# Gate and up products of the FFN by one level of Strassen's seven-product scheme, in a float32 decoder layer on one NeuronCore

## The chip, the cores and the metric

The kernel runs on one NeuronCore of a Trainium2 chip. The metric is the device time of one execution in microseconds; the number given for a kernel is the median of its runs. The engines of the core are TensorE (PE in the profile), VectorE (DVE), ScalarE (ACT), GpSimd (POOL) and SyncE (SP), which issues most of the DMAs. Each runs its own program, and they wait for each other by semaphores. Times of the profile are counted from the start of its span.

## The reference, cut to what matters

One layer of a decoder with 512 prompt tokens and 8 sample tokens, D_MODEL = 2048 and D_FF = 5632:

```python
def layer_out(h, o_sb, o_cm, p, g_out_sb, g_out_cm, w_out, g_ffn, w_gate, w_up, w_down,
              g_ple, w_ple_gate, w_ple_proj):
    ...
    h = h + o @ w_out
    f = rmsnorm(h, g_ffn)
    h = h + (jax.nn.silu(f @ w_gate) * (f @ w_up)) @ w_down
    h = h + jax.nn.sigmoid(rmsnorm(h, g_ple) @ w_ple_gate) * (p @ w_ple_proj)
    return h
```

Ahead of it stand an input projection, a stick-breaking attention group (with 8 x 1024 cached positions) and a gating group, called the mixer here. The change leaves their work as it is. `p` has 256 features.

## The kernel before

**Layout.** All activations lie feature-major: `h`, `x_hi` and `x_lo` are 128 x 16 x 520, that is KT = 16 k-tiles of 128 features by TOK = 520 tokens, which are taken as two halves of HALF = 260. A float32 product is made of three float32r products, `w_hi`·`x_hi`, `w_hi`·`x_lo` and `w_lo`·`x_hi`; the high part is a copy on ScalarE rounded to float32r, the low part a subtraction on VectorE.

**Weights** come in units of 16 blocks of 128 x 128 (1 MB). SP loads them into `w_raw` (two slots), ScalarE makes `w_hi` by halves (`split_w`, `high_w`, L611), VectorE `w_lo` (`low_w`, L868). A unit is 16 blocks x 3 terms x 2 token halves = 96 matmuls of 260 columns (L1214) on TensorE (`unit`), which go into `out_ps`, two tiles in turn (`tile_ps`), each of two PSUM banks, one for each token half. A tile is taken off before the tile after the next starts (`out_read`).

**Order of the program.** Units 0 to 55 are the mixer and the output projection, whose results VectorE adds to `h` (L985). TensorE then sums the squares of `h` over the features by four matmuls with `ones` (`sum_features`, L1253) from `h_sum`, which POOL has added up (L591); this gives `h_r`, the reciprocal root. The FFN has 11 chunks of four 128-feature tiles: per chunk 8 units gate and up, 4 units down (16 output tiles of 4 blocks, 24 matmuls each). The chunks are shifted: the gate and up units of a chunk stand ahead of the down units of the chunk before. The first chunk's gate and up and the last chunk's down are written out, the ten between are a hardware loop of 5 iterations of 24 units on each engine (`Fori`).

**Gate and up** use `h`·gain as operand; VectorE multiplies the finished tile by `h_r` (`take_loop`, L1131) into `y_gate` and `y_up`, ScalarE makes silu, VectorE the product and `act_lo` (`gate_up`). **Down:** VectorE adds each tile to `h` in SBUF (`down_tile`, L1156). **After the FFN** two units multiply `p` (proj, 16 tiles of two blocks), which VectorE copies to SBUF. Then 16 units form the PLE gate, each taken by VectorE (L892), put through the sigmoid, multiplied by proj (L1202), added to `h` (L1203) and stored (`y_t`, L478). While the last down tiles come, VectorE makes the operand of the gate from them (`low_x`), so that between two tiles it has one addition and at times a `low_w` and a `low_x`.

## Time and profile before

| | us |
|---|---|
| median of 3 runs | 2661.23 |
| lowest and highest run | 2659.47, 2663.26 |
| profiled execution, its own time | 2663.89 |
| span of the profiled execution | 2662.3 |
| mean granted clock of TensorE, share of full speed | 0.994 |

The profile is of one execution: a page with the busy time of each engine and its costliest groups, the chain of work that ended last followed back from the end, every instruction with its start and length, and the idle time ahead of it with the instruction that ended it (`<-`). 2663.89 less 2662.3 leaves 1.6 us outside the span. The granted clock is that of TensorE alone; 0.50 is 1.2 GHz and 1.00 is 2.4 GHz.

### The profile page before, as it was taken

Reading aid. Unit: us, or ns where it says so; the run is one execution under the profiler, and the core shown is the slowest. Engines: PE = TensorE matmul, PEld = TensorE weight load, DVE = VectorE, ACT = ScalarE, POOL = GpSimd, SP = SyncE. Lnnn points to the kernel's source line nnn. Section 1 sums busy time; section 2 is a strip of 40 time slices with the busy share of each in tenths; the row PEclk is TensorE's granted clock in tenths of the full one; section 3 lists DMA queues with packets and bytes.
Section 4 is the critical chain, followed back from the end, with each engine's and each line's share of the span. In section 5 each row is a group of like instructions: output and inputs, shape, how many; then the busy total and the mean of one; then the engine's idle time right before and its main releaser. Section 6 shows DMA issues by size and latency. Waiting matters only on the chain.

```text
span 2662.3 us, 49219 instructions
## 1 busy us (share of the span) xinstructions
PE 2623.2 (99%) x21484; PEld 2600.7 (98%) x21484; DVE 1218.7 (46%) x1400; ACT 781.3 (29%) x912; POOL 158.2 (6%) x170
## 2 busy tenths in 40 slices
PE   7999999999999999999999999999999999999999
PEld 6998999999999999999999999999999999999999
DVE  6368776554456533333333333334343424346443
ACT  5544434444523322222122212121212121224221
POOL 4001111110111200000000000000000000003000
PEclk9998999999999999999999999999999999999999
DMA  4255565554332222222222222222222222222223
GB/s 177 95 190 190 215 237 207 175 186 160 108 128 100 84 96 95 85 91 96 96 82 93 96 80 96 96 96 81 95 96 92 93 86 96 94 83 94 96 86 106
DMA packets 57389, 309.18 MB, mean 116 GB/s; under 512 B 7770, under 2 KB 7770, under 8 KB 30178
## 3 DMA queue, kind: packets, MB, share of 16 engines
q1 hardware_dynamic: 47826, 272.50, 29.0%
q0 software_dynamic: 9216, 33.56, 3.6%
q8 instruction: 177, 2.90, 0.4%
q14 instruction: 26, 0.21, 0.0%
q10 hardware_dynamic: 144, 0.01, 0.0%
HBM read 297.46 MB, written 8.59 MB: 115 GB/s over the span
## 4 chain that ended last, share of the span: by engine, by line
PE 95%; DVE 3%; DMA 1%; ACT 1%; issue 1%; SPq 0%; DVEq 0%; ACTq 0%
PE out_ps L1214 87%; PE out_ps L1336 4%; PE pair_ps L1253 1%; DVE w_lo L868 1%; DVE k_ring L899 0%; PE tok_ps L1321 0%; DVE dot_s L900 0%; DMA q_rows<-q_rows_dram 0%; DMA h<-x_t 0%; ACT x_hi L622 0%; PE pair_ps L1284 0%; PE pair_ps L1303 0%; PE tok_ps L1317 0%; PE pair_ps L1290 0%; PE pair_ps L1299 0%
## 5 line engine op out<-in xcount | busy, mean ns | idle before, releaser
L1214 PE MATMUL out_ps<-x_hi,w_hi 128*128 128x260 f32 x5184 | 1066.9, 287 | 25.8 <-DVE w_lo L868 10.0
L1214 PE MATMUL out_ps<-x_hi,w_lo 128*128 128x260 f32 x5184 | 1048.6, 284 | 0.0
L1214 PE MATMUL out_ps<-x_lo,w_hi 128*128 128x260 f32 x5184 | 1046.8, 284 | 0.0
L1214 PEld LDWEIGHTS out_ps<-x_hi,w_hi 128*128 128x128 f32 x5184 | 805.8, 190 | 31.8 <-DVE w_lo L868 8.9
L1214 PEld LDWEIGHTS out_ps<-x_hi,w_lo 128*128 128x128 f32 x5184 | 803.6, 189 | 0.0
L1214 PEld LDWEIGHTS out_ps<-x_lo,w_hi 128*128 128x128 f32 x5184 | 801.4, 189 | 0.0
L611 ACT ACTIVATE w_hi<-w_raw 128x1024 fp32r<-128x1024 f32 x412 | 411.7, 1047 | 590.2 <-PE out_ps L1214 590.2
L868 DVE TENSOR_TENSOR w_lo<-w_raw,w_hi 128x1024 fp32r<-128x1024 f32 x410 | 501.4, 1255 | 125.1 <-ACT w_hi L611 123.7
L1214 PE MATMUL out_ps<-act_hi,w_lo 128*128 128x260 f32 x1408 | 283.9, 283 | 0.0
L1214 PE MATMUL out_ps<-act_lo,w_hi 128*128 128x260 f32 x1408 | 283.3, 283 | 0.0
L1214 PE MATMUL out_ps<-act_hi,w_hi 128*128 128x260 f32 x1408 | 283.2, 282 | 0.0
L1156 DVE TENSOR_TENSOR h<-h,out_ps 128x520 f32<-128x520 f32 x176 | 122.3, 695 | 228.2 <-PE out_ps L1214 228.1
L1214 PEld LDWEIGHTS out_ps<-act_hi,w_lo 128*128 128x128 f32 x1408 | 217.1, 188 | 0.0
L1214 PEld LDWEIGHTS out_ps<-act_hi,w_hi 128*128 128x128 f32 x1408 | 217.1, 188 | 0.0
L1214 PEld LDWEIGHTS out_ps<-act_lo,w_hi 128*128 128x128 f32 x1408 | 216.6, 188 | 0.0
L1131 DVE TENSOR_TENSOR y_up<-out_ps,h_r 128x520 f32<-128x520 f32 x44 | 30.8, 700 | 295.6 <-PE out_ps L1214 295.6
L1131 DVE TENSOR_TENSOR y_gate<-out_ps,h_r 128x520 f32<-128x520 f32 x44 | 30.8, 700 | 285.0 <-PE out_ps L1214 285.0
L818 ACT ACTIVATE act_hi<-y_up 128x520 fp32r<-128x520 f32 x44 | 28.1, 639 | 428.2 <-DVE y_up L1148 428.2
L815 ACT ACTIVATE y_gate<-y_gate 128x520 f32<-128x520 f32 x44 | 28.1, 640 | 381.5 <-DVE y_gate L1131 381.5
L593 POOL COPY h_sum<-h_sq 128x520 f32<-128x520 f32 x2 | 1.8, 902 | 1543.8 <-ACT h_sq L691 1543.8
L1336 PEld LDWEIGHTS out_ps<-a_s,v_ring 128*128 128x128 f32 x688 | 82.1, 195 | 0.0
L1336 PE MATMUL out_ps<-a_s,v_ring 128*128 128x1 f32 x688 | 80.7, 247 | 0.0
(175 smaller groups left out, 1366.0 us busy)
## 6 DMA issues: line engine op xcount, KB each, us to landing
w_raw<-w_units SPq DMA_DIRECT2D x205, 1024.0 KB, 4.8
k_ring<-cache_k SPq DMA_DIRECT2D x50, 512.0 KB, 5.2
v_ring<-cache_v POOLq DMA_DIRECT2D x43, 512.0 KB, 4.5
acc<-cache_v POOLq DMA_DIRECT2D x21, 512.0 KB, 4.8
k_third<-cache_k SPq DMA_DIRECT2D x14, 512.0 KB, 4.5
h<-x_t SPq DMA_DIRECT2D x4, 1040.0 KB, 9.5
y_t<-h SPq DMA_DIRECT2D x16, 260.0 KB, 6.5
q_rows<-q_rows_dram SPq DMA_DIRECT2D x8, 512.0 KB, 5.4
```

Of the source, the lines that this page charges most:

```text
L593: ins = pool.tensor_copy(h_sum[:, :], h_sq[:, 0, :])
L611: act.activation(w_hi[:, u % 2, cols], w_raw[:, u % 2, cols], ACT.Copy).then_inc(hi_done, 1)
L815: act.activation(y_gate[:, :], y_gate[:, :], ACT.Silu).then_inc(silu_done, 1)
L818: act.activation(act_hi[:, par, g, :], y_up[:, :], ACT.Copy).then_inc(act_hi_done, 1)
L868: dve.tensor_tensor(w_lo[:, u % 2, cols], w_raw[:, u % 2, cols], w_hi[:, u % 2, cols], ALU.subtract).then_inc(lo_done, 1)
L1131: dve.tensor_tensor(halves(dst), tile_ps(t), halves(h_r[:, :]), ALU.mult).then_inc(out_read, 1)
L1156: dve.tensor_tensor(halves(h[:, m, :]), halves(h[:, m, :]), tile_ps(t), ALU.add)\
L1214: mm = pe.matmul(out_ps[:, 2 * (t % 2) + a, 0:HALF], w[:, u % 2, cols], x[:, a * HALF:(a + 1) * HALF], start=first and n == 0, stop=last a ...
L1253: mm = pe.matmul(pair_ps[:, a, 0:HALF], ones[:, :], x[:, a * HALF:(a + 1) * HALF], start=True, stop=True)
L1336: mm = pe.matmul(o_s_ps(u)[:, hd:hd + 1], v_slot(j)[:, hd * P:(hd + 1) * P], a_s[:, b % 3, at:at + 1], start=False, stop=j == pages[-1], s ...
```

## The change

**Products.** Two output tiles (2 x 128 features) of gate or up, the two halves of K (8 k-tiles each) and the two token halves form a 2 x 2 by 2 x 2 block product. It is made with seven block products in place of eight (Winograd's form). One block product is 8 k-tiles x 3 terms = 24 matmuls of 260 columns; a pair of tiles takes 168 matmuls where it took 192, and there are 44 pairs (22 gate, 22 up). `product` issues one, `pair_of_tiles` on each engine one pair. Their results go into six single PSUM banks (`gate_acc`, `up_acc`), all matmuls of a product into one bank.

**Operands.** The seven token operands (`ops` 0 to 6, high and low parts of 128 x 8 x 260) stay in SBUF through the FFN. They are built once, from `f` = `h`·gain (ScalarE), multiplied by `h_r` (`scale_op`), combined (`combine_op`), rounded (`high_op`) and subtracted (`low_op`). The weight operands are made anew for each pair: VectorE adds four half units (`add_weights`) and makes seven low parts, ScalarE seven high parts, four copies of a partial result (`copy_part`) and VectorE three additions (`join`). Weights now go by half units ("jobs", four half slots of `w_hi` and `w_lo`); a third raw slot, `w_extra`, is added. The second load of a pair waits for the sums of the pair before, since sums are made in place.

**Residual.** `h` gives its place in SBUF to operands. SP stores it tile by tile to `h_dram` during the last 8 units of the output projection and after them. Each down tile of the first ten chunks is copied by ScalarE into one of four `staging` buffers and added to `h_dram` by a DMA that POOL issues with `accum_op=ALU.add` (160 of 128 x 520 float32, 260 KB). Ahead of the last down, `h` comes back in four loads of 1040 KB, and VectorE adds the last chunk's tiles to it in SBUF.

**Projection** of `p`: its 16 tiles (192 matmuls) move ahead of the FFN; ScalarE copies each to one of two `staging` buffers, POOL stores it to `proj_dram`, and it is loaded back in two halves for the PLE gate.

**Also:** `h_r` comes from Ln and Exp instead of Sqrt and a reciprocal, and ScalarE's table sets are loaded ahead in more places and 28 times instead of 89. The loop has one chunk an iteration: ten iterations on TensorE instead of five.

The diff, cut:

```diff
+            for k in range(KT - 2, KT):
+                keep_h(k)
+            def after_low(job, it=0):
+                sp.wait_ge(lo_done, it * CHUNK_JOBS + (JOB0 + job + 1 - POOL_LO))
+            def after_sums(pair, it=0):
+                sp.wait_ge(w_summed, it * 16 + 4 * (pair + 1))
...
+            sp.wait_ge(ended, LAST_DOWN.end - 2)
+            for i in range(STAGES):
+                sp.wait_ge(h_added[i], 64 * (FFN_CHUNKS - 1))
+            for i in range(4):
+                tiles = slice(4 * i, 4 * i + 4)
+                sp.dma_start(h[:, tiles, :], h_dram[:, tiles, :]).then_inc(h_back[i], 16)
...
+            for n in range(KT):
+                pool.wait_ge(proj_taken, n + 1)
+                pool.dma_start(proj_dram[:, n, :], staging[:, n % 2, :]).then_inc(proj_out[n % 2], 16)
+            for c in range(FFN_CHUNKS - 1):
+                for m in range(KT):
+                    pool.wait_ge(staged, c * KT + m + 1)
+                    pool.dma_start(h_dram[:, m, :], staging[:, m % STAGES, :], accum_op=ALU.add)\
+                        .then_inc(h_added[m % STAGES], 16)
...
+            def take_proj(n):
+                act.wait_ge(ended, n + 1)
+                if n >= 2:
+                    act.wait_ge(proj_out[n % 2], 16 * (n // 2))
+                act.activation(halves(staging[:, n % 2, :]), tile_ps(n), ACT.Copy).then_inc(proj_taken, 1)
...
+            def down_tiles(item, after, it):
+                for j in range(2 * FFN_GROUP):
+                    for t in range(2 * j, 2 * j + 2):
+                        after_end(item.end + t + 1, it)
+                        if t >= STAGES:
+                            act.wait_ge(h_added[t % STAGES], it * 64 + 16 * (t // STAGES))
+                        act.activation(halves(staging[:, t % STAGES, :]), tile_ps(t), ACT.Copy).then_inc(staged, 1)
+                    if j < 4:
+                        high_of(item, j + 4, it)
+                    else:
+                        high_of(after, j - 4, it)
...
+            high_of(first, 1)
+            for g in range(2):
+                high_op(2, g, quad(0, 0, g), 8)
+                take_proj(8 + g)
+            take_proj(10)
+            take_proj(11)
+            high_of(first, 2)
+            for i in range(STAGES):
+                act.wait_ge(h_kept[i], 64)
+            for g in range(2):
+                high_op(3, g, quad(1, 0, g), 12)
+                take_proj(12 + g)
...
+            for j in range(2 * FFN_GROUP):
+                after_end(LAST_DOWN.end + 2 * j + 2)
+                if j < 4:
+                    high_of(LAST_DOWN, j + 4)
+                else:
+                    high_gate(j - 4)
+                for k in range(2 * j, 2 * j + 2):
+                    act.wait_ge(taken, k + 1)
+                    split(x_hi[:, k, :], h[:, k, :], gain_ple[:, k:k + 1])
                     if k >= 2:
-                        split(x_hi[:, k, :], h[:, k, :], gain_ple[:, k:k + 1])
-                    square_residual(KT, k)
-            split_w(U_PROJ + 1)
...
+                    if stage:
+                        low_raw(item.job + stage - 1, item.load + (stage - 1) // 2, (stage - 1) % 2, it)
+                elif stage == 0:
+                    dve.wait_ge(*landed(item.load + 1, it))
+                    after_low(item.job - 2, it)
+                    add_weights(w_sum[:, :], half_of(item.load + 1, 0), half_of(item.load + 1, 1))
+                elif stage == 1:
+                    low_raw(item.job, item.load, 0, it)
+                elif stage == 2:
+                    low(item.job + 1, w_sum[:, :], it)
+                    dve.wait_ge(w_summed, it * 16 + (4 * item.pair + 1))
+                    add_weights(half_of(item.load + 1, 0), half_of(item.load, 0), half_of(item.load + 1, 0))
+                    after_low(item.job + 1, it)
+                    add_weights(w_sum[:, :], w_sum[:, :], half_of(item.load, 0))
+                elif stage == 3:
+                    low(item.job + 2, w_sum[:, :], it)
...
-            def down_tile(t, m, it=0):
-                dve.wait_ge(out_done, it * (2 * CHUNK_TILES) + (t + 1))
-                dve.wait_ge(out_read, it * (2 * CHUNK_TILES) + t)
-                dve.tensor_tensor(halves(h[:, m, :]), halves(h[:, m, :]), tile_ps(t), ALU.add)\
-                    .then_inc(out_read, 1)
...
+                dve.wait_ge(ended, it * CHUNK_ENDS + (item.end + 4))
+                dve.wait_ge(copied, it * 16 + (4 * item.pair + 1))
+                join(part[:, 0, :], part[:, 0, :], y_acc)
+                prepare(after, 1, it)
+                dve.wait_ge(copied, it * 16 + (4 * item.pair + 4))
+                join(part[:, 2, :], part[:, 2, :], part[:, 3, :])
+                prepare(after, 2, it)
...
+            def scale_op(half_k, half_t, g):
+                x = quad(half_k, half_t, g)
+                r = h_r[:, half_t * HALF:(half_t + 1) * HALF].unsqueeze(1).to_broadcast([P, 4, HALF])
+                dve.tensor_tensor(x, x, r, ALU.mult).then_inc(op_built, 1)
...
+            first = FIRST[0]
+            prepare(first, 0)
+            dve.wait_ge(root_done, 4)
+            dve.wait_ge(f_done, KT)
+            for g in range(2):
+                scale_op(0, 0, g)
...
+            for j in range(2 * FFN_GROUP):
+                if j < 4:
+                    low_raw(LAST_DOWN.job + j + 4, LAST_DOWN.load + (j + 4) // 2, j % 2)
+                else:
+                    low_gate(j - 4)
+                for k in range(2 * j, 2 * j + 2):
+                    if k % 4 == 0:
+                        dve.wait_ge(h_back[k // 4], 16)
+                    dve.wait_ge(ended, LAST_DOWN.end + k + 1)
+                    dve.tensor_tensor(halves(h[:, k, :]), halves(h[:, k, :]), tile_ps(k), ALU.add).then_inc(taken, 1)
+                    if k:
+                        low_x(k - 1, h[:, k - 1, :], gain_ple[:, k - 1:k])
...
+            def product(job, op, acc, fresh, it=0):
+                after_low(job, it)
+                hi, lo = ops[op]
+                for g in range(GROUPS):
+                    if job < FIRST[1].job and g % 4 == 0:
+                        pe.wait_ge(op_lo_done, 2 * op + g // 4 + 1)
+                    cols = slice(g * P, (g + 1) * P)
+                    w_h, w_l = half_slot(w_hi, job)[:, cols], half_slot(w_lo, job)[:, cols]
+                    for n, (w, x) in enumerate(((w_h, hi), (w_h, lo), (w_l, hi))):
+                        mm = pe.matmul(acc, w, x[:, g, :], start=fresh and g == 0 and n == 0,
+                                       stop=g == GROUPS - 1 and n == 2, skip_group_check=True)
+                mm.then_inc(ended, 1)
...
+                    pe.wait_ge(up_read if up else gate_read, it * 2 + turn_of)
+                    pe.wait_ge(joined, it * 12 + 3 * (item.pair - 1))
+                product(item.job, 0, x_acc, True, it)
+                product(item.job + 1, 1, z_acc, True, it)
+                pe.wait_ge(copied, it * 16 + (4 * item.pair + 1))
+                product(item.job + 2, 2, x_acc, False, it)
+                product(item.job + 3, 3, y_acc, True, it)
+                pe.wait_ge(copied, it * 16 + (4 * item.pair + 3))
+                product(item.job + 4, 4, x_acc, False, it)
+                product(item.job + 5, 5, z_acc, False, it)
+                pe.wait_ge(copied, it * 16 + (4 * item.pair + 4))
+                product(item.job + 6, 6, x_acc, False, it)
...
+            pe.wait_ge(p_lo_done, 2)
+            for n in range(KT):
+                job = n // 4
+                if n % 4 == 0:
+                    after_low(job)
+                if n < 2:
+                    pe.wait_ge(out_read, T_FFN - 1 + n)
+                else:
+                    pe.wait_ge(proj_taken, n - 1)
+                for k in range(2):
+                    plain_block(job, n % 4 * 2 + k, tile_ps(n), p_hi[:, k, :], p_lo[:, k, :], k == 0, k == 1)
+                if n == 2:
                     sum_features(h_sum, h_sum_done, KT, (root_done, 4)).then_inc(x_sum_ready, 1)
...
-            with pe.Fori(0, (FFN_CHUNKS - 1) // 2) as it:
-                for half in range(2):
-                    u0 = U_LOOP + half * CHUNK_UNITS
-                    for x in range(2 * FFN_GROUP):
-                        unit(u0 + x, 1, ffn_operand, it=it)
-                    pe.wait_ge(act_lo_done, it * (2 * FFN_GROUP) + FFN_GROUP * (1 + half))
...
+            with pe.Fori(0, FFN_CHUNKS - 1) as it:
+                g0, down, u0, g1, u1 = LOOP
+                pair_of_tiles(g0, gate_acc, it)
+                pe.wait_ge(act_lo_done, it * 2 + 2)
+                pe.wait_ge(joined, it * 12 + 3 * (g0.pair))
+                down_tiles(down, lambda t: pe.wait_ge(staged, it * KT + (t - 1)) if t >= 2 else None, it)
+                pe.wait_ge(staged, it * KT + KT)
+                pair_of_tiles(u0, up_acc, it)
+                pair_of_tiles(g1, gate_acc, it)
+                pair_of_tiles(u1, up_acc, it)
+            pe.wait_ge(act_lo_done, 2 * FFN_CHUNKS)
+            pe.wait_ge(joined, 3 * 4 * FFN_CHUNKS)
```

VectorE's order where the FFN begins; `w_lo`, `op_lo` and `f` are the low parts of weights and operands and the residual times gain. Before:

```order
L985 TENSOR_TENSOR h<-h,sq 128x520 [waits out_read]
L877 SCALAR_TENSOR_TENSOR x_lo<-h,gain_ffn,x_hi 128x520 [waits x_hi_done,h_final]
L877 SCALAR_TENSOR_TENSOR x_lo<-h,gain_ffn,x_hi 128x520 [waits x_hi_done] x7
L868 TENSOR_TENSOR w_lo<-w_raw,w_hi 128x1024 [waits hi_done] x2
L882 RECIPROCAL h_r<-h_r 128x520 [waits root_done]
L1131 TENSOR_TENSOR y_gate<-out_ps,h_r 128x520 [waits out_done,r_done]
L868 TENSOR_TENSOR w_lo<-w_raw,w_hi 128x1024 [waits hi_done] x2
```

After the change:

```order
L1351 TENSOR_TENSOR h<-h,sq 128x520 [waits out_read]
L1234 TENSOR_TENSOR w_lo<-w_raw,w_hi 128x1024 [waits hi_done,h_final]
L1234 TENSOR_TENSOR w_lo<-w_raw,w_hi 128x1024 [waits hi_done]
L1512 TENSOR_TENSOR w_sum<-w_raw 128x1024 [waits lo_done,w_in0]
L1591 TENSOR_TENSOR f<-f,h_r 128x4x260 [waits f_done,root_done]
L1591 TENSOR_TENSOR f<-f,h_r 128x4x260 x3
L1499 TENSOR_TENSOR w_lo<-w_extra,w_hi 128x1024 [waits hi_done]
L1603 TENSOR_TENSOR op_lo<-f,op_hi 128x1040 [waits op_hi_done] x2
L1596 SCALAR_TENSOR_TENSOR f<-f 128x4x260 [waits op_built] x2
L1591 TENSOR_TENSOR f<-f,h_r 128x4x260 x2
L1603 TENSOR_TENSOR op_lo<-f,op_hi 128x1040 [waits op_hi_done] x2
L1499 TENSOR_TENSOR w_lo<-w_sum,w_hi 128x1024 [waits hi_done]
```

Between the last addition to `h` and the steady work stood eight `x_lo`, a unit's two low parts and the reciprocal; now the same place holds the building of the seven operands (instructions on `f` and `op_lo`) with the weight work of the first pair between them.

VectorE in the last down phase, from its first `w_lo`. Before:

```order
L868 TENSOR_TENSOR w_lo<-w_raw,w_hi 128x1024 [waits hi_done]
L1156 TENSOR_TENSOR h<-h,out_ps 128x520 [waits out_read,out_done]
L868 TENSOR_TENSOR w_lo<-w_raw,w_hi 128x1024 [waits hi_done]
L1156 TENSOR_TENSOR h<-h,out_ps 128x520 [waits out_read,out_done] x3
L877 SCALAR_TENSOR_TENSOR x_lo<-h,gain_ple,x_hi 128x520 [waits x_hi_done]
L868 TENSOR_TENSOR w_lo<-w_raw,w_hi 128x1024 [waits hi_done]
L1156 TENSOR_TENSOR h<-h,out_ps 128x520 [waits out_read,out_done]
L877 SCALAR_TENSOR_TENSOR x_lo<-h,gain_ple,x_hi 128x520 [waits x_hi_done]
```

After the change:

```order
L1499 TENSOR_TENSOR w_lo<-w_raw,w_hi 128x1024 [waits hi_done]
L1676 TENSOR_TENSOR h<-h,out_ps 128x520 [waits ended,h_back0]
L1676 TENSOR_TENSOR h<-h,out_ps 128x520 [waits ended]
L1243 SCALAR_TENSOR_TENSOR x_lo<-h,gain_ple,x_hi 128x520 [waits x_hi_done]
L1499 TENSOR_TENSOR w_lo<-w_raw,w_hi 128x1024 [waits hi_done]
L1676 TENSOR_TENSOR h<-h,out_ps 128x520 [waits ended]
L1243 SCALAR_TENSOR_TENSOR x_lo<-h,gain_ple,x_hi 128x520 [waits x_hi_done]
L1676 TENSOR_TENSOR h<-h,out_ps 128x520 [waits ended]
L1243 SCALAR_TENSOR_TENSOR x_lo<-h,gain_ple,x_hi 128x520 [waits x_hi_done]
```

A `w_lo` now stands ahead of every two additions to `h` to the end of the phase, each made when ScalarE has the high part (`hi_done`).

TensorE at the end of a down phase in the loop, its last block and the next gate or up product. Before:

```order
L1214 MATMUL out_ps<-act_lo,w_hi 128x260 x2
L1214 MATMUL out_ps<-act_hi,w_lo 128x260 x2
L1226 REGISTER_ALU
L1233 REGISTER_ALU [waits lo_done]
L1214 MATMUL out_ps<-x_hi,w_hi 128x260 [waits out_read]
```

After the change:

```order
L1919 MATMUL out_ps<-act_lo,w_hi 128x260 x2
L1919 MATMUL out_ps<-act_hi,w_lo 128x260 x2
L1995 REGISTER_ALU
L1911 REGISTER_ALU [waits joined,up_read,staged]
L1934 MATMUL mix_ps<-op_hi,w_hi 128x260 [waits lo_done]
```

The first matmul of the next product waited for the tile before the last one to be taken (`out_read`, a count); now a register instruction ahead of it waits for all sixteen staging copies (`staged`).

## Rows read from the trace of the kernel before

**Rows 1.** The page: busy time of each engine (part 1).
```profile
PE 2623.2 (99%) x21484; PEld 2600.7 (98%) x21484; DVE 1218.7 (46%) x1400; ACT 781.3 (29%) x912; POOL 158.2 (6%) x170
```

**Rows 2.** The chain that ended last, from 915 us: start, length, what.
```profile
914.99 12.12 PE out_ps L1214 x101
927.11 0.88 PE pair_ps L1253 x4
...
2472.31 184.53 PE out_ps L1214 x1536
```

**Rows 3.** VectorE in order of time as the FFN begins (start, duration).
```profile
916.42 0.70 DVE L985 TENSOR_TENSOR h<-h,sq 128x520 f32<-128x520 f32 x1
...
951.16 0.70 DVE L1131 TENSOR_TENSOR y_gate<-out_ps,h_r 128x520 f32<-128x520 f32 x1 [6.15 <-PE out_ps L1214]
953.52 2.36 DVE L868 TENSOR_TENSOR w_lo<-w_raw,w_hi 128x1024 fp32r<-128x1024 f32 x2 [1.66 <-ACT w_hi L611]
...
974.23 0.70 DVE L1131 TENSOR_TENSOR y_gate<-out_ps,h_r 128x520 f32<-128x520 f32 x1 [6.15 <-PE out_ps L1214]
```

**Rows 4.** Busy time in stretches (columns in its first line): loop turns, after two waits.
```profile
core 0: us, PE busy (x) PEld busy (x) DVE busy (x) ACT busy (x) POOL busy (x), PEclk, DMA share, GB/s
1275.00:1295.00 20.00, 18.44 (x154) 18.24 (x154) 7.51 (x8) 3.08 (x4) 0.00 (x0) 1.00 0.31 107
1555.00:1575.00 20.00, 18.21 (x140) 18.01 (x139) 6.29 (x8) 2.00 (x2) 0.00 (x0) 0.91 0.31 107
...
52.00:53.00 1.00, 1.00 (x6) 1.00 (x6) 0.00 (x0) 0.24 (x1) 0.00 (x0) 0.50 0.00 0
...
55.00:56.00 1.00, 1.00 (x10) 1.00 (x10) 0.00 (x0) 0.00 (x0) 0.00 (x0) 1.00 0.00 0
...
253.00:254.00 1.00, 1.00 (x5) 1.00 (x6) 0.93 (x3) 0.00 (x0) 0.00 (x0) 0.50 0.07 16
262.00:263.00 1.00, 1.00 (x7) 1.00 (x6) 0.50 (x1) 0.00 (x0) 0.00 (x0) 0.50 0.98 295
```

**Rows 5.** TensorE in order of time: matmuls that followed a wait (last bracket).
```profile
50.42 0.48 PE L1214 MATMUL out_ps<-x_hi,w_hi 128*128 128x260 f32 x2 [2.33 <-DVE y L892]
...
252.92 1.10 PE L1265 MATMUL tok_ps<-ident,vg 128*128 128x128 f32 x4 [2.99 <-DVE vg L1064]
...
1287.08 0.50 PE L1214 MATMUL out_ps<-x_hi,w_hi 128*128 128x260 f32 x2 [1.56 <-DVE h L1156]
```

**Rows 6.** VectorE, groups of instructions by line and shape: busy us, mean ns.
```profile
L868 DVE TENSOR_TENSOR w_lo<-w_raw,w_hi 128x1024 fp32r<-128x1024 f32 x410 | 501.4, 1255 | 125.1 <-ACT w_hi L611 123.7
...
L886 DVE SCALAR_TENSOR_TENSOR q<-y,gain_q,sq 128x520 f32<-128x520 f32 x8 | 6.1, 760 | 38.8 <-ACT sq L636 38.8
...
L999 DVE TENSOR_TENSOR x_sq<-x_sq 128x1040 f32<-128x1040 f32 x4 | 5.0, 1239 | 0.1
...
L972 DVE TENSOR_TENSOR z<-z,mix_ps 128x256 f32<-128x256 f32 x8 | 3.4, 420 | 0.3
```

**Rows 7.** VectorE late in the last down phase (in order of time).
```profile
2415.95 1.56 DVE L868 TENSOR_TENSOR w_lo<-w_raw,w_hi 128x1024 fp32r<-128x1024 f32 x1 [1.60 <-ACT w_hi L611]
2417.43 0.68 DVE L1156 TENSOR_TENSOR h<-h,out_ps 128x520 f32<-128x520 f32 x1
```

**Rows 8.** ScalarE, groups by line, 850 to 1010 us.
```profile
L611 ACT ACTIVATE w_hi<-w_raw 128x1024 fp32r<-128x1024 f32 x26 | 26.0, 1048 | 38.6 <-PE out_ps L1214 38.6
...
L815 ACT ACTIVATE y_gate<-y_gate 128x520 f32<-128x520 f32 x4 | 2.6, 638 | 27.9 <-DVE y_gate L1131 27.9
...
L627 ACT ACTIVATE h_r<-pair_ps,eps 128x520 f32<-128x520 f32 x1 | 0.7, 697 | 4.4 <-PE pair_ps L1253 4.4
```

**Rows 9.** The page: DMA issues, median us to landing (part 6).
```profile
w_raw<-w_units SPq DMA_DIRECT2D x205, 1024.0 KB, 4.8
```

**Rows 10.** Landing times of the 16 y_t stores and of the 8 k_t stores.
```profile
DMA to landing us min/median/max: 2.0/6.5/7.1
...
DMA to landing us min/median/max: 6.2/6.7/8.1
```

More of the change, by code:

```diff
@@ L57 @@
 U_GATE = U_PROJ + 2
-UNITS = U_GATE + KT
 T_OUT = U_OUT
@@ new lines, in _ @@
+            for i in range(2):
+                sp.wait_ge(proj_out[i], 16 * HEADS)
+            sp.wait_ge(ended, LAST_DOWN.end)
+            sp.dma_start(proj[:, 0:HEADS, :], proj_dram[:, 0:HEADS, :]).then_inc(proj_in_done[0], 16)
+            for i in range(LAST_DOWN.load + 3, GATE_LOAD + KT):
+                after_low(LAST_DOWN.job + 2 * (i - RAW_SLOTS - LAST_DOWN.load) + 1)
+                load(i, U_LAST_DOWN + 3 if i < GATE_LOAD else U_GATE + i - GATE_LOAD)
+                if i == GATE_LOAD + 2:
+                    sp.wait_ge(ended, GATE_END)
+                    sp.dma_start(proj[:, HEADS:KT, :], proj_dram[:, HEADS:KT, :]).then_inc(proj_in_done[1], 16)
@@ new lines, in high_op, with after_end, high, high_raw @@
+            def high_op(i, g, src, built_at):
+                act.wait_ge(op_built, built_at + g + 1)
+                act.activation(ops[i][0][:, 4 * g:4 * g + 4, :], src, ACT.Copy).then_inc(op_hi_done, 1)
+            def after_end(end, it=0):
+                act.wait_ge(ended, it * CHUNK_ENDS + end)
+            def high(job, src):
+                act.activation(half_slot(w_hi, job), src, ACT.Copy).then_inc(hi_done, 1)
+            def high_raw(job, i, half, it=0):
+                act.wait_ge(*landed(i, it))
+                high(job, raw(i)[:, half * GROUPS * P:(half + 1) * GROUPS * P])
@@ new lines, in half_of, with add_weights, prepare @@
+            def half_of(i, half):
+                return raw(i)[:, half * GROUPS * P:(half + 1) * GROUPS * P]
+            def add_weights(dst, x, w):
+                dve.tensor_tensor(dst, x, w, ALU.add).then_inc(w_summed, 1)
+            def prepare(item, stage, it=0):
+                if isinstance(item, Down):
+                    if stage:
[14 more added lines that the diff above has]
+                    low(item.job + 2, w_sum[:, :], it)
+                else:
+                    low_raw(item.job + 3, item.load, 1, it)
+                    after_low(item.job + 2, it)
+                    add_weights(w_sum[:, :], w_sum[:, :], half_of(item.load, 1))
@@ L1218, in block_products, with unit @@
                     mm.then_inc(out_done, 1)
-            def unit(u, tiles, operand, each=None, it=0, between={}):
+            def unit(u, tiles, operand, each=None, between={}):
                 per = SLOTS // tiles
@@ new lines, in plain_block @@
+            def plain_block(job, b, tile, hi, lo, first, last):
+                cols = slice(b * P, (b + 1) * P)
+                w_h, w_l = half_slot(w_hi, job)[:, cols], half_slot(w_lo, job)[:, cols]
+                for n, (w, x) in enumerate(((w_h, hi), (w_h, lo), (w_l, hi))):
+                    for a in range(2):
+                        mm = pe.matmul(tile[:, a, :], w, x[:, a * HALF:(a + 1) * HALF],
+                                       start=first and n == 0, stop=last and n == 2)
+                if last:
+                    mm.then_inc(ended, 1)
```

707 lines of the change are left out of this document (503 added, 204 removed).

## Prediction

> **What bounds the kernel now.** I read the page's busy times first: TensorE is busy 2623.2 of 2662.3 us, VectorE 46% and ScalarE 29% [rows 1]. The chain that ended last then names matmuls nearly throughout, one stretch without a break being 1536 matmuls in 184.53 us, 120.1 ns each [rows 2]. So what leaves TensorE's program leaves the time, and what makes TensorE wait is added. Last come the stretches around its few waits: a turn of the loop costs 1.56 us [rows 5], and after a wait the granted clock can stand at half (1.2 GHz) for a while [rows 4]. The times below are on the profiled execution, 2663.9 us with 1.6 outside the span.
>
> **Removed.** 44 pairs lose 24 matmuls each, 1056 x 120.1 ns = **126.9 us**. Down, gate and the 192 matmuls of proj stay as many. That a matmul costs the same when all of a product go into one bank is not shown before, where two banks alternate; the nearest row, four alternating matmuls in 0.88 us, tells little [rows 2], so I take 120.1 for both. A bound: 5 ns either way on the 7392 matmuls of the products would be 37 us. I see no reason for either sign.
>
> The Trainium skill (TensorE: Matmul & The Clock Gate, Back-to-back issue gap) gives N/2.4 + 2.5 ns for an isolated matmul of N columns, 110.8 ns for 260. The trace has 120.1, so the row decides; by the page the saving would be 117.0.
>
> **Steady work, hidden.** A product is 24 x 0.1201 = 2.88 us, a pair 20.18. VectorE does 11 instructions of 1024 elements per pair; two back to back take 2.36 us [rows 3], 1.18 each, and 1.255 as the group's mean [rows 6]. With three joins near the 256-column row's 0.42 this is 14.2 us for a gate pair. For an up pair come a 520-column product (0.70), two of 260 columns from PSUM (near 0.42) and a 1040-column subtraction (1.24), 17.1 in all [rows 3, 6]. ScalarE has seven highs at 1.05 and four copies, about 10 [rows 8]. Both fit in 20.18, and following the waits product by product I find each low part ready over 4 us early. The third raw slot lets the second load of a pair go at about 4.8 us into the pair before; it lands 4.8 later [rows 9], at 9.6, and is first read at 11.3. Down tiles take 2.88 each; ScalarE needs 2 x 0.65 + 1.05 = 2.35 of 5.77 per two tiles [rows 8]. What this cover lacks: VectorE has only 3 us to spare in an up pair.
>
> **Building the operands: +23.1.** Let 0 be the end of the output projection, 915.6 us in the trace: two units of gate and up lie between the two takes at 951.16 and 974.23, so a unit is 11.53 [rows 3]. TensorE alone would do proj (23.07), the sums (0.88 [rows 2]) and pair 0 (20.18) by 44.1. But VectorE has 38 large instructions (scales, combinations and low parts of 1040 elements, weight sums and low parts of 1024) before product 4 may start. They are near 1.24 and 1.18 each [rows 3, 6], 1.18 taken: 44.8. They begin when the last addition is done (1.5: it starts at 916.42 and takes 0.70 [rows 3]), the root is there (sums at 7.9, Ln and Exp 0.70 and 0.64 like the 520-column rows [rows 8], so 9.3), and the load issued after the last store of h has landed (about 10, two loads of 4.8 in a row [rows 9]); I take 11.1. So low part 4 is ready at 56, products 4 to 6 end at 64.7, and the excess is 20.6. In it TensorE waits twice, near 5 and 7 us, for proj tiles whose copies stand behind ScalarE's `high_op`; after waits of 2.33 and 2.99 us the clock stood at half [rows 4, 5]. I put 2.5 on it. Bounds: at 1.24 each the chain is 2.3 longer, and eight of its instructions do two operations, which at 520 columns take 0.76 [rows 6], twice that 1.52: 2.7 more. If a proj store lands as late as a y_t store in a row of them (7.1 us, 2.0 when alone [rows 10]), two takes cycle in 7.9 and it is +18 more; downwards the two clock losses and a load that lands at 8 allow -4.5.
>
> **Loop turns: +10.** Nine turns instead of four, 1.56 us each [rows 5], and one of the four seen stood at a granted clock of 0.91 over 20 us, the others near 1.00 [rows 4], 1.8 us lost in one of four. So 2.0 each, and five more are 10; 0 to 3 each is the range.
>
> **End of each down phase: +8.** TensorE waits there for the sixteenth staging copy: the copy of 520 columns, 0.64 [rows 8], and the two handovers, 0.8. Ten times. Before, it went on with another tile pair.
>
> **Before the last down: +3.5.** The last up pair's products end, then two short multiplications, a low part ahead of them, ScalarE's high and VectorE's low of the activations (1.24 [rows 6]) must pass before the first down block; part of it overlaps. From 2 to 5.
>
> **The last down: +24.** Before, VectorE's `w_lo` of 1.56 us waited 1.60 for ScalarE's high part and the addition of 0.68 came after it [rows 7]; the slot of that unit was free a unit early. Now ScalarE may write the high part of job j+4 only when tile 2j+1 ends, VectorE's low of it stands ahead of the additions of tiles 2j and 2j+1, and tile 2j+2 waits for the first of these. TensorE's gap is high 1.05 [rows 8], low 1.18 [rows 3], addition 0.70 [rows 3] less overlap, with handovers 3.0. Eight times. Bounds 2.0 and 3.9 each, so 16 and 31.
>
> **The clock after these nine gaps: +14.4.** The nearest rows: after the wait of 2.33 us that ended at 50.42 the clock is 0.50 at 52 to 53 and 1.00 at 55; I read 3.2 us at half, 1.6 lost. After one of 2.99 that ended at 252.92 it is still 0.50 at 262 to 263, some 10 us, 5.1 lost [rows 4, 5]. The gaps here are 3.0 but the work between them, 5.8 us, is dense; and a turn of 1.56 cost nothing three times in four. I take 1.6 each; 0 and 5.1 each are the bounds, 0 and 46.
>
> **Sum:** 23.1 + 10 + 8 + 3.5 + 24 + 14.4 = 83.0 against 126.9, net -43.9: 2663.9 - 43.9 = 2620.0. The profiled run is 2.7 above the median, so **2617** for the median.
>
> **Rivals.**
>
> *The accumulating DMA paces the down phases, slower than before.* Tile t is copied only when the DMA of tile t-4 has landed. With copy and handover 0.7 and landing time L, four slots hold if (0.7 + L)/4 is at most 2.88 us, L at most 10.8 us. ScalarE, waiting for it, also holds back `high_of` queued behind it, and POOL's queue holds only these. The trace has no accumulating DMA. Plain transfers of the same 260 KB landed in 2.0 to 7.1 and the k_t stores in 6.2 to 8.1 [rows 10], which is for the cover. An addition in DRAM reads the old value beside the new one, so as the far end I take twice the row's 7.1, 14.2: a tile then takes 3.73 instead of 2.88: 160 x 0.85 = 136, so 2617 + 136 = **2753**. It turns the result over from L = 11.9, where 160 x 0.27 = 44. Against it: the DMA engines are little used in the FFN, and one DMA at a time was the fast case.
>
> The Trainium skill (Collectives: The Full Stack, The bandwidth ceiling) says that a transfer with an add needs two source reads and runs at half the rate. No row of the kernel before shows whether that holds here.
>
> *The clock stays low, or proj's stores hold the prologue.* Nine gaps at 5.1 instead of 1.6 give +31.5: **2648**. The stores at 7.1 give +18: 2635; both 2667.
>
> *The gaps are smaller.* No clock lost at the nine (-14.4), the last down's gap at 2.0 (-8) and turns of 1.56 as before (-4): **2591**.
>
> *The change doesn't do what it says*, TensorE's count of matmuls not falling by 1056: excluded by the instruction order but for the price of each; 5 ns more on each product matmul gives 2654.
>
> **How the numbers follow.** Main case 0.52, 2595 to 2645. Clock or stores 0.14, 2645 to 2667. Smaller gaps 0.17, 2575 to 2600. Slow accumulating DMA 0.14, 2656 to 2753. The rest 0.03. The range takes in all but the low tail of the third (0.05) and most of the fourth (0.12): 2580 to 2680. The measurement of this kernel tells 0.2% (5.3 us) from no change. Below 2655.9 lie the first, the third and nearly all of the second case: 0.82. Within 0.2%: 0.03. Above 2666.6: 0.15.
>
> **What would show it.** TensorE's matmul records: 1056 fewer, at 120 ns in an unbroken stretch of products. Product 4 of the first pair starting near 56 us after the output projection's end, ended by an `op_lo`. In the loop's down phases, the median landing time of the accumulating DMAs under 10.8, and no TensorE wait released by ScalarE's staging copy but at the end of each. In the last down, eight waits of 3 us released by the addition to h, and the granted clock around them. I am wrong if the pairs in the loop take clearly more than 20.2 us, if the down phases take over 46 + 1 us, or if the loads come late for `add_weights`.

## The result and the profile after

| | before | after |
|---|---|---|
| median, us | 2661.61 (4 runs, 2659.47 to 2663.26) | 2616.66 (4 runs, 2613.26 to 2622.05) |
| profiled execution, its time and span | 2663.89, 2662.3 | 2618.02, 2616.1 |
| mean granted clock | 0.994 | 0.984 |

The ratio of the times is 0.9831, with a 95% interval of 0.9818 to 0.9843: 45 us faster. The forecast was 2617. In the profiled executions the stretch from the end of the output projection to the end of the span shrank by 43.9 us (1746.7 to 1702.8), which is the forecast's net to the digit. That is luck in part: below, the matmuls saved 6 us more than forecast, and the waits with the clock cost 7 more.

The page of the changed kernel, busy time by engine (it answers to [rows 1]):

```profile
PE 2520.4 (96%) x20428; PEld 2492.4 (95%) x20428; DVE 1450.2 (55%) x1588; ACT 1015.5 (39%) x1351; POOL 304.2 (12%) x346
```

TensorE's records fell from 21484 to 20428, by 1056. It is no longer busy all the time: 96% instead of 99%. Its waits, summed by the instruction that waited and the one that released it (us, times, longest):

```profile
PE out_ps L1919 <- DVE h L1676: 24.7, 8, 3.1
PE out_ps L1919 <- ACT staging L1020: 13.1, 7, 5.6
PE pair_ps L1934 <- DVE w_lo L1499: 10.4, 6, 1.9
...
PE mix_ps L1934 <- ACT staging L1117: 7.7, 10, 0.8
...
PE pair_ps L1934 <- issue: 4.4, 3, 1.5
PE out_ps L1919 <- DVE act_lo L1574: 3.6, 1, 3.6
```

These lines are the forecast's terms: eight waits for the addition to `h` in the last down phase, seven for the projection's copies, nine at the turns of the loop (six ended by `w_lo`, three by nothing that shows, "issue"), ten for the sixteenth staging copy, one for `act_lo`. In order of time, TensorE after one wait of each kind (idle time in the last bracket):

```profile
1105.51 0.38 PE L1934 MATMUL mix_ps<-op_hi,w_hi 128*128 128x260 f32 x1 [0.77 <-ACT staging L1117]
...
1167.92 0.38 PE L1934 MATMUL pair_ps<-op_hi,w_hi 128*128 128x260 f32 x1 [1.82 <-DVE w_lo L1499]
...
2337.74 0.51 PE L1919 MATMUL out_ps<-act_hi,w_hi 128*128 128x260 f32 x2 [3.56 <-DVE act_lo L1574]
...
2348.40 0.48 PE L1919 MATMUL out_ps<-act_hi,w_hi 128*128 128x260 f32 x2 [3.10 <-DVE h L1676]
...
2423.54 0.51 PE L1919 MATMUL out_ps<-x_hi,w_hi 128*128 128x260 f32 x2 [3.01 <-DVE h L1676]
```

From 2337.74 to 2423.54 are 85.8 us for 384 matmuls that take 45.88 without a wait. The chain that ended last shows both rates (start, length, what): 72 matmuls of products in 8.62 us are 119.7 ns each, 384 of a down phase in 45.88 are 119.5, and the first product after the turn took 4.66 instead of 2.87:

```profile
1058.87 45.88 PE out_ps L1919 x384
...
1131.63 8.62 PE pair_ps L1934 x72
...
1167.92 4.66 PE pair_ps L1934 x24
```

The granted clock (the column after the busy times of PE, PEld, DVE, ACT and POOL, as in [rows 4]) in that first product, and in a block of the last down phase after its wait:

```profile
1169.00:1171.00 2.00, 2.00 (x11) 2.00 (x11) 2.00 (x3) 0.49 (x1) 0.00 (x0) 0.50 0.00 0
...
2369.70:2372.00 2.30, 2.30 (x11) 2.30 (x12) 1.75 (x3) 2.28 (x4) 1.07 (x1) 0.51 0.03 7
```

### The profile page after: what moved, and what is told of

It is laid out like the page before. It is cut to its first block, busy times and chain, and to the rows that moved or that the text cites. A ratio compares the mean times of both kernels' runs of the same rounds, so it can differ in the third digit from the quotient of the medians.

```text
span 2616.1 us, 48548 instructions
## 1 busy us (share of the span) xinstructions
PE 2520.4 (96%) x20428; PEld 2492.4 (95%) x20428; DVE 1450.2 (55%) x1588; ACT 1015.5 (39%) x1351; POOL 304.2 (12%) x346
## 3 DMA queue, kind: packets, MB, share of 16 engines
q0 software_dynamic: 33536, 80.43, 15.2%
## 4 chain that ended last, share of the span: by engine, by line
PE 90%; DVE 5%; ACT 2%; issue 2%; DMA 2%; SPq 0%; DVEq 0%; POOL 0%; ACTq 0%; POOLq 0%
PE out_ps L1919 27%; PE out_ps L1702 22%; PE pair_ps L1934 12%; PE mix_ps L1934 9%; PE out_ps L1934 7%; PE tok_ps L1934 5%; PE out_ps L1824 4%; PE pair_ps L1741 1%; ACT w_hi L1033 1%; DVE x_lo L1243 1%; DVE w_lo L1499 1%; DVE dot_s L1266 1%; DVE w_lo L1234 1%; DVE k_ring L1265 1%; DMA k_ring<-cache_k 0%
## 5 line engine op out<-in xcount | busy, mean ns | idle before, releaser
L1702 PE MATMUL out_ps<-x_hi,w_hi 128*128 128x260 f32 x1792 | 383.5, 296 | 17.8 <-DVE w_lo L1234 9.6
L1499 DVE TENSOR_TENSOR w_lo<-w_raw,w_hi 128x1024 fp32r<-128x1024 f32 x196 | 239.0, 1223 | 276.6 <-ACT w_hi L1033 276.6
L1702 PE MATMUL out_ps<-x_hi,w_lo 128*128 128x260 f32 x1792 | 364.8, 285 | 0.0
L1702 PE MATMUL out_ps<-x_lo,w_hi 128*128 128x260 f32 x1792 | 364.4, 285 | 0.0
L1702 PEld LDWEIGHTS out_ps<-x_hi,w_hi 128*128 128x128 f32 x1792 | 282.5, 192 | 22.4 <-DVE w_lo L1234 9.1
L1702 PEld LDWEIGHTS out_ps<-x_hi,w_lo 128*128 128x128 f32 x1792 | 280.5, 191 | 0.0
L1702 PEld LDWEIGHTS out_ps<-x_lo,w_hi 128*128 128x128 f32 x1792 | 280.0, 191 | 0.0
L1934 PE MATMUL pair_ps<-op_hi,w_hi 128*128 128x260 f32 x880 | 250.5, 285 | 15.7 <-DVE w_lo L1499 10.4
L1934 PE MATMUL pair_ps<-op_hi,w_lo 128*128 128x260 f32 x880 | 250.5, 285 | 0.0
L1934 PE MATMUL pair_ps<-op_lo,w_hi 128*128 128x260 f32 x880 | 250.0, 284 | 0.0
```

The lines of the kernel that those rows point to most:

```text
L1499: dve.tensor_tensor(half_slot(w_lo, job), src, half_slot(w_hi, job), ALU.subtract)\
L1702: mm = pe.matmul(out_ps[:, 2 * (t % 2) + a, 0:HALF], w[:, u % 2, cols], x[:, a * HALF:(a + 1) * HALF], start=first and n == 0, stop=last a ...
L1934: mm = pe.matmul(acc, w, x[:, g, :], start=fresh and g == 0 and n == 0, stop=g == GROUPS - 1 and n == 2, skip_group_check=True)
```

## The experiments

All are edits of the changed kernel and are compared with its 2616. One thing is needed to read the small effects: the output projection, which no edit touches, ended between 909.3 and 918.4 us of the span in the profiled executions, so a whole time says little about 3 us. For such effects I read stretches inside a trace.

**The changed kernel again.**

> The changed kernel once more, as the reference for the small effects of the runs beside it. Every theory: 2616 +- 4 us, TensorE's waits in the last down phase 8 of 3.1 us, at the end of the loop's down phases 10 of 0.77, at the loop turns 9 of 1.5 to 1.9.

2615.88 (2612.89 to 2621.56, 5 runs). The loop's period, from one wait for the sixteenth copy to the next over nine chunks, was 129.4 us, 129.8 in the first trace. The waits at the turns are as long in both; the granted clock fell after three of the nine turns in the first trace and after one of nine in this one, and each such turn made its period 1.4 to 1.9 us longer.

**Last down phase: additions ahead of the low part (adds_first).**

```diff
             for j in range(2 * FFN_GROUP):
-                if j < 4:
-                    low_raw(LAST_DOWN.job + j + 4, LAST_DOWN.load + (j + 4) // 2, j % 2)
-                else:
-                    low_gate(j - 4)
                 for k in range(2 * j, 2 * j + 2):
...
                     dve.tensor_tensor(halves(h[:, k, :]), halves(h[:, k, :]), tile_ps(k), ALU.add).then_inc(taken, 1)
+                    if k % 2:
+                        if j < 4:
+                            low_raw(LAST_DOWN.job + j + 4, LAST_DOWN.load + (j + 4) // 2, j % 2)
+                        else:
+                            low_gate(j - 4)
```

> In the last down phase VectorE adds tiles 2j and 2j+1 to h before it makes the low part of job j+4, instead of after it. Theory (the order of VectorE's queue makes the gaps): the eight waits of 3.1 us go (24.7), and with them the time at half clock after them. From the changed kernel's trace that stretch lasts 85.8 us from the start of its first block to the first gate block, less 46 of work less 24.7 is 15; one share of it, near 2, stays behind the wait for act_lo. So -38 us: 2579. Rival 1 (the low part is as urgent as the addition): TensorE then waits about 1 us eight times for w_lo, the clock still drops: 2600. Rival 2 (the low clock in this stretch has another cause than the waits): only the 24.7 go: 2592.

2577.16 (2574.77 to 2579.84), 38.7 less. The waits for `h` are gone from TensorE's list; what is left after the loop is the one for `act_lo`:

```profile
PE mix_ps L1935 <- ACT staging L1117: 7.7, 10, 0.8
...
PE out_ps L1920 <- DVE act_lo L1574: 3.6, 1, 3.6
```

24.7 of the 38.7 are the waits, 14 the time at the low clock, which went with them: the stretch of 85.8 us now takes 48.4, and the gate after it 1.6 less. Neither rival holds: no `w_lo` took their place, and the low clock left with the waits, but for the 2.5 us that follow the wait for `act_lo`.

**Fifteen staging copies (staged_15).**

```diff
-                pe.wait_ge(staged, it * KT + KT)
+                pe.wait_ge(staged, it * KT + KT - 1)
```

> TensorE waits at the end of each of the ten down phases for fifteen staging copies instead of sixteen; the banks of tile 14 are those the next product pair uses, tile 15's are not. Theory (the wait is for ScalarE's last copy and nothing else is late there): ten waits of 0.77 go and 0.1 each with them: 2608. Rival (the next product's low part or ScalarE's up_read is as late): under 2 us, 2615.

2605.60 (2601.97 to 2612.75), 10.3 less than the run beside it (2615.88), where the theory had 8 and the rival under 2. The waits for the copies are gone from the list, and the loop's shortest period fell from 129.1 to 128.1 us: 1.0 for each wait of 0.77. The other 0.3 is not the clock, which stood at 1.00 after all ten of these waits; what it is was not tried.

**TensorE's loop written out (no_loop).**

```diff
-            with pe.Fori(0, FFN_CHUNKS - 1) as it:
+            for it in range(FFN_CHUNKS - 1):
```

> TensorE's loop over ten chunks is written out (about 10,000 more matmuls in its program); the other engines keep their loops. Theory (a turn costs TensorE 1.5 to 1.9 us, and some turns a stretch at half clock): the iterations took 129.1 us, five of them 131, so 9 x 1.6 and 5 x 1.9 go, 24: 2593. Rival 1 (the wait at the turn is VectorE's w_lo, which the trace names as releaser in five of nine): the wait stays there, about 1 us five times, 2602. Rival 2 (a long straight program starves TensorE for instructions): 2616 or more.

2597.06 (2594.22 to 2598.59), 18.8 less, 5 short of the theory and as far from the first rival. The trace decides between them: no wait is left at the former turns, and the period is flat.

```profile
1236.28 0.39 PE L1934 MATMUL mix_ps<-op_hi,w_hi 128*128 128x260 f32 x1 [0.69 <-ACT staging L1117]
...
1363.58 0.39 PE L1934 MATMUL mix_ps<-op_hi,w_hi 128*128 128x260 f32 x1 [0.69 <-ACT staging L1117]
```

127.29 us apart, as all nine are. Against the 129.43 of the run beside it that is 2.1 us a turn and 19.3 in all, which is the 18.8 measured; against the 129.79 of the first trace, with two more turns at the low clock, it is 2.5 and 22.5. The theory had taken five long turns of nine; the first trace has three and the run beside it one. So `w_lo`, which the trace named as releaser at most turns, was not what TensorE lacked there, and rival 1 falls. And a straight program of some 10,000 matmuls is fed without a wait.

**The projection ahead of the operands (proj_early).**

```diff
-                pool.dma_start(proj_dram[:, n, :], staging[:, n % 2, :]).then_inc(proj_out[n % 2], 16)
+                pool.dma_start(proj_dram[:, n, :], staging[:, n % 3, :]).then_inc(proj_out[n % 3], 16)
...
+            for n in range(8, 11):
+                take_proj(n)
             high_of(first, 1)
+            for n in range(11, 14):
+                take_proj(n)
             for g in range(2):
                 high_op(2, g, quad(0, 0, g), 8)
-                take_proj(8 + g)
-            take_proj(10)
-            take_proj(11)
+                take_proj(14 + g)
```

> The sixteen tiles of p's projection go through three staging buffers instead of two, and ScalarE copies tiles 8 to 15 ahead of the high parts of operands 2 to 4 instead of between them. From the end of the output projection the first down phase began 145.5 to 146.4 us later in five runs of kernels with the old order. Theory (VectorE's chain of 38 instructions, which ended 55.5 us after that point, ties with TensorE's delayed projection): TensorE's waits of 13 us and most of the time at half clock move to a wait for VectorE's low parts, and the stretch shortens by about 1 us: 144.5, the whole 2615. Rival (the stores and ScalarE's copies alone hold this stretch, as the chain of waits reads): it shortens by the 13 us of waits and some 5 us of clock, 128 us, the whole 2598.

2615.32 (4 runs), and the stretch from the end of the output projection (909.8) to the first down phase (1059.7) took 150.0 us, 4.5 more than before the edit. TensorE's waits for the projection's copies fell from 13.1 to 7.4 us, but now it waited 11.8 at product 2, for ScalarE's copy of an earlier result (`part`). That copy stood in ScalarE's queue behind the last high parts of the operands, which waited 4.49 us for VectorE's `op_lo`. And VectorE's chain was 3.5 us longer, since ScalarE's high part of job 1 stood behind the copies I had moved. First VectorE, then ScalarE and TensorE:

```profile
939.86 1.23 DVE L1499 TENSOR_TENSOR w_lo<-w_sum,w_hi 128x1024 fp32r<-128x1024 f32 x1 [3.68 <-ACT w_hi L1033]
...
960.65 2.03 ACT L1025 ACTIVATE op_hi<-f 128x1040 fp32r<-128x1040 f32 x2 [4.49 <-DVE op_lo L1603]
...
963.01 0.58 PE L1934 MATMUL pair_ps<-op_hi,w_hi 128*128 128x260 f32 x1 [11.81 <-ACT part L1066]
```

In size both expectations missed. In kind it is the theory's case: TensorE's earlier work became a wait, and the stretch followed VectorE's chain, by way of ScalarE's queue. Product 4 itself did not wait for its low part, which was ready 2 us before it started.

**All together (combined).** The four edits above, and the low parts of operands 5 and 6 behind those of weight jobs 4 and 5 (VectorE's part shown):

```diff
                 low(item.job + 4, half_of(item.load + 1, 0), it)
+                if opening:
+                    for g in range(2):
+                        low_op(5, g, quad(1, 1, g))
                 low(item.job + 5, w_sum[:, :], it)
+                if opening:
+                    for g in range(2):
+                        low_op(6, g, quad(1, 0, g))
```

> Adds first, fifteen staging copies, no loop on TensorE and the early projection together, and beside these the low parts of operands 5 and 6 behind the low parts of weight jobs 4 and 5 on VectorE, their high parts likewise on ScalarE. Theory (the terms add up): from 2616, 38.7, 10.3 and, by the loop's period in the trace, 2.5 x 9 = 22.5 less; VectorE reaches the low part of job 4 four instructions earlier, 4.7 us: 2539. Rival (the terms overlap: with one wait gone the next is late): about half of them, 2575.

2547.44 (2543.37 to 2553.78): 69 of 77 us. The stretch ahead of the first down phase was 146.0 where the theory had it 4.7 shorter than 145.4; that is 5 of the missing 8, and most of the rest is that the loop's turns were counted at 2.5 us instead of 2.1. VectorE waited 2.2 us for the high part of job 1 here, not the 3.7 of proj_early.

**All together, one instruction moved (combined_2).**

> The combined kernel with one instruction moved: ScalarE's high part of job 1 stands ahead of its copies of projection tiles 8 to 10. In proj_early and combined VectorE waited some 3.5 us for it in the middle of its chain, and the stretch from the output projection's end to the first down phase was 150.0 us in proj_early against 145.5. Theory (VectorE's chain holds this stretch): 3.5 us less than in combined, whose stretch was 145.7: 142; the whole 2544, which is no more than the spread of the runs. Rival (the stretch is held by stores and copies of the projection): no change of the stretch.

```diff
-            for n in range(8, 11):
-                take_proj(n)
             high_of(first, 1)
-            for n in range(11, 14):
+            for n in range(8, 14):
                 take_proj(n)
```

2544.92 (2543.17 to 2549.54, 5 runs), a ratio of 0.9564 to before, interval 0.9548 to 0.9579; the stretch was 143.5, 2.5 less. The theory had 3.5, the rival none. The theory had carried the loss over from proj_early: against this run VectorE's chain in combined was 2.5 us late, and the stretch shortened by just that. So the chain holds the stretch. It is not alone, though: against the changed kernel the low part of job 4 is ready 5.0 us earlier and the stretch only 1.9 shorter, and TensorE still waits once for VectorE's `w_lo` and three times for ScalarE's copies of partial results (the third, of 1.4, into `mix_ps`).

```profile
PE out_ps L1921 <- ACT staging L1020: 7.4, 4, 3.9
...
PE pair_ps L1936 <- DVE w_lo L1499: 2.7, 1, 2.7
...
PE pair_ps L1936 <- ACT part L1066: 2.2, 2, 1.3
```

```profile
PE 2492.6 (98%) x20428; PEld 2469.0 (97%) x20428; DVE 1453.6 (57%) x1588; ACT 1012.8 (40%) x1351; POOL 307.2 (12%) x346
```

Its loop has a period of 126.3 us, all of it matmuls.

**A product made twice (eight_products).** `extra` leaves out the signal at the first one's end.

```diff
+                product(item.job + 1, 1, z_acc, True, it, extra=True)
                 product(item.job + 1, 1, z_acc, True, it)
```

> Each pair of tiles makes one product twice (24 matmuls more in each of 44 pairs, the first result is overwritten), all else as changed. Theory (TensorE bounds the pairs and every matmul costs 120 ns): 1056 x 0.1197 = 126.4 us more: 2742. Rival (VectorE or ScalarE is near to being late in the up pairs and gets slack by this): clearly less than 126, about 100, 2716. Were a matmul of a product that goes into one bank dearer than the old alternating ones, more than 127.

2762.61 (2758.72 to 2764.64), 146 more, outside the theory and the rival. As a number it would fit a dearer matmul, but in the chain the doubled product costs what it should, 48 matmuls in 5.75 us:

```profile
1428.48 5.75 PE tok_ps L1934 x48
```

The other 20 us are at the loop's turns. At each of the nine TensorE waited twice, the second time inside the first product and for nothing that shows, 25.5 us in all where the changed kernel has 14.8, and after five of them the granted clock fell:

```profile
1473.08 0.38 PE L1934 MATMUL pair_ps<-op_hi,w_hi 128*128 128x260 f32 x1 [1.50 <-DVE w_lo L1499]
...
1476.23 0.58 PE L1934 MATMUL pair_ps<-op_hi,w_lo 128*128 128x260 f32 x1 [1.57 <-issue]
```

The period was 143.4 us where 129.8 and four products of 2.87 make 141.3: 2.1 us more in each, 19 in nine. A loop body with 96 more matmuls pays more at its turn. Why was not tried.

**Two staging buffers (two_slots).**

```diff
-                        if t >= STAGES:
-                            act.wait_ge(h_added[t % STAGES], it * 64 + 16 * (t // STAGES))
-                        act.activation(halves(staging[:, t % STAGES, :]), tile_ps(t), ACT.Copy).then_inc(staged, 1)
+                        if t >= 2:
+                            act.wait_ge(h_added[t % 2], it * 128 + 16 * (t // 2))
+                        act.activation(halves(staging[:, t % 2, :]), tile_ps(t), ACT.Copy).then_inc(staged, 1)
```

> Two staging buffers instead of four between the down tiles' copies and the accumulating DMAs. They landed in 4.4 us (median; 3.8 to 9.5). With two, (0.65 + L)/2 must be at most 2.88, L at most 5.1. Theory (the price of this rival is as worked out, the median decides and most tiles still fit): 0 to 15 us more, 2616 to 2631, with waits of TensorE for staging at the few late landings. Rival (landing time grows with the load or has a long tail in each phase): L near 7, 0.95 us a tile, 150 us more, 2766.

2666.02 (2661.10 to 2671.23, 10 runs), 50 more, which is all that the change had gained. The median landing was 4.9 us, under the 5.1 that two buffers allow, but it ranges from 3.9 to 8.4, 64 of the 160 landed later than 5.1, and the late ones cost:

```profile
PE out_ps L1919 <- ACT staging L1117: 28.5, 23, 2.5
...
PE mix_ps L1934 <- ACT staging L1117: 12.6, 10, 1.8
```

28.5 and 4.9 more than before at the phase ends make 33; the period is 134.7 instead of 129.8, 49 us in ten, so some 16 us are not these waits. About 7 of them are the clock: over the loop, time at half clock cost 12 us here and 5 in the changed kernel; the rest was not taken apart. The rule with the median was too mild by 35 us. The rival had the tail right and its size, L near 7, wrong. The trace of the changed kernel could have told: 66 of its 160 landings were already over 5.1.

**Stores in place of additions (plain_store).**

```diff
-                    pool.dma_start(h_dram[:, m, :], staging[:, m % STAGES, :], accum_op=ALU.add)\
+                    pool.dma_start(h_dram[:, m, :], staging[:, m % STAGES, :])\
```

> The 160 DMAs of the down tiles write over h_dram instead of adding to it, so the residual of the first ten chunks is left out; all else as changed. They landed in 4.4 us with the addition. Theory (an addition costs the DMA something, and four buffers hide it): 2616, no change, landing at 2.3 to 4, as proj's stores of the same size landed in 2.3 when alone. Rival 1 (the addition itself is free and 4.4 is what the down phase's load makes of any store): landing 4.4, the whole unchanged. Rival 2 (late landings cost TensorE time already): 5 us or more faster.

2616.25 (2614.76 to 2617.45): no change. The landing times, without the addition and then with it (the changed kernel):

```profile
DMA to landing us min/median/max: 2.3/2.3/7.1
```

```profile
DMA to landing us min/median/max: 3.8/4.4/9.5
```

2.3 against 4.4 us: the addition costs 2.1 us a tile in the median, and four buffers hide it. The Trainium skill (Collectives: The Full Stack, The bandwidth ceiling) has the adding step of a ring collective at half the rate of the copying one, since the addition reads two sources. It says so of ring collectives and not of a single transfer; here the median landing times stand as 1.9 to 1, the means (5.3 and 3.2 us) as 1.6 to 1.

## Why the prediction was right, step by step

| term | forecast | measured |
|---|---|---|
| 1056 matmuls fewer | -126.9 | -126.9 by the price of before |
| price of the products' matmuls | 0 | -3.3 |
| price of the down phases' matmuls | 0 | -2.8 |
| building the operands | +23.1 | +21.0 |
| loop turns | +10 | +13.0 |
| end of ten down phases | +8 | +9.6 |
| before the last down | +3.5 | +3.6 |
| last down, waits | +24 | +24.7 |
| clock after the nine waits | +14.4 | +17.8 |

**Removed:** right. A product made twice is 2.87 us more. A matmul of a product, into one bank with its neighbours, takes 119.7 ns where one of the old units took 120.1; on 7392 that is 3.3 us. A matmul of a down phase takes 119.48 after the change and took 120.14 before (the last 768 of them in 92.3 us without a wait), on 4224 another 2.8 us. Down blocks still use two banks in turn, so the single bank is not shown to be the reason; I had no term for either. The 5 ns of my bound are not reached, and neither is the 110.8 ns that I worked out from the Trainium skill (TensorE: Matmul & The Clock Gate, Back-to-back issue gap) for an isolated matmul.

**Building the operands:** the size was right (65.1 us to the end of pair 0; forecast 64.7), and VectorE's chain of 38 instructions had the low part of job 4 at 55.5 (56). The step "product 4 starts near 56, ended by an `op_lo`" was wrong: it started at 56.3 without a wait. TensorE had by then lost 13.1 us to the projection's copies and 0.9 to ScalarE's copy of a result, where I had two waits and 2.5 us for their clock; the other 7 of the 21.0 are mostly time at half clock (the mean granted clock of these 65.1 us is 0.90). No `op_lo` cost TensorE anything. The size came out right because VectorE's chain, from which I had worked it out, ended within 1 us of TensorE's own delays, and not because TensorE waited for its low parts; that is luck in part. The chain that ended last reads as if the projection's stores were the cause:

```profile
920.10 7.55 DMA proj_dram<-staging
...
943.30 1.16 DVE f L1596
...
946.10 4.79 PE out_ps L1919 x24
...
963.77 8.90 PE pair_ps L1934 x72
```

A first store took 7.55 us of it. Two chains ended within 1 us of each other; the view shows the one that ended last, and proj_early shows that taking it away alone gains nothing.

**Loop turns:** the term was 3 us too small. In this trace a turn costs 2.5 us (22.5 in nine, against no_loop's period), 1.5 to 1.9 of it the wait and most of the rest the clock, which fell after three of the nine; I had 2.0. Before, the kernel spent 1556.7 us from the output projection to the gate (from 915.6 to 2472.3 [rows 2]). Its 8448 gate and up matmuls, the 4224 of down and the 192 of proj at 120.14, with two sums of 0.88, make 1547.2. That leaves 9.5 us for its four turns and all edges, where I had taken off 8. In the second trace of the changed kernel, with one fall of the clock, the same term is 9.8: it moves by 3 us between executions.

**End of the down phases, before the last down, last down:** right, 0.77 for 0.8, 3.56 for 3.5, 3.10 for 3.0.

**The clock after nine waits:** 2.0 each where I took 1.6, and the bound of 5.1 was not reached once. After the eight waits the blocks of the last down began 10.4 to 11.9 us apart, where 5.74 and a wait of 3.10 make 8.84: 15.2 in the whole phase. The gate then took 2.6 us more than the 16 units and the tail of before. After each of the nine waits of 3 us the clock fell, after a turn in three of nine, after the ten waits of 0.77 never.

**Rivals:** the slow accumulating DMA did not come; its median landing of 4.4, and its latest of 9.5, lie under 10.8. That the mechanism exists, two_slots shows; its price by one landing time for all was too mild there. The smaller gaps and the longer low clock did not come. Of the signs named, the pairs in the loop took 20.1 us, the down phases 45.9, and only the end of each down phase waited for a staging copy.

Summed, waits and clock are 89.7 where I had 83.0, and the matmuls 133.0 less where I had 126.9: net -43.3 by the terms, -43.9 in the spans. The mechanism was as predicted in every term but the building of the operands; the agreement to the digit rests on two misses of 6 to 7 us that cancel.

## What to carry to other kernels

Where one engine bounds, work removed from it counts in full only if it brings no new wait: here 127 us removed gave 45. Three edits of a few lines gave 38.7, 10.3 and 18.8 more, in the order of one queue, in one count, in a loop's turn; with the reordered opening they reach 2544.9 together. An instruction that waits for a slow partner must not stand ahead of one that frees what the bounding engine needs. Before an experiment on one chain, look for a second that ends nearly with it. Count how many transfers land later than the buffers allow, not whether their median does.

## What the runs showed of the hardware

- Each wait of TensorE of 3.1 us was followed by some 2 us lost at half the clock (0.51 in the row above): waits of 24.7 us cost 38.7 (adds_first). After the ten waits of 0.77 us in the same trace the granted clock stayed at 1.00, after the nine waits of 1.5 to 1.9 it fell three times.
- A turn of TensorE's hardware loop costs 1.5 to 1.9 us of idle and, written out, nothing (no_loop); with a body of 96 matmuls more it cost 2.1 us more again (eight_products).
- A DMA of 260 KB that adds in DRAM landed in 4.4 us, without the addition in 2.3 (medians, plain_store); the latest landings were 9.5 and 7.1 us.
